# Attention masks as one-pass operands, and the gate as second factor of the normalising instruction

## The reference, cut to what matters

```python
# forgetting attention of the first layer, 128-wide heads
s = jnp.where(pos_k[None, :] <= pos_q[:, None], s, -jnp.inf)
p = jax.nn.softmax(s, axis=-1)
# selected attention: the 256 best keys of an index score
score = jnp.where(k_pos[None, None, :] <= q_pos[None, :, None], score, NEG_INF)
_, idx = lax.top_k(score, n_top)
# stick breaking: keys strictly before the query
mask = k_pos[None, :] < q_pos[:, None]
```

## Time and profile before

| | |
|---|---|
| median of 3 runs | 3654.83 us |
| the runs | 3655.05, 3650.49, 3654.83 us |
| the profiled execution | 3650.83 us |
| its span | 3649.1 us |
| PE, DVE, ACT, POOL busy | 3427.9, 1545.9, 1270.9, 321.0 us |
| mean granted clock of PE | 0.959 |

### The profile page before, as it was taken

One profiled execution on the slowest core, in us unless ns is written; L12 is line 12 of the kernel. 1 busy time (PEld: TensorE's weight loads), 2 busy tenths in 40 slices (PEclk: granted clock), 3 DMA queues, 4 the chain that ended last, 5 costly groups with the idle time before them and its releaser, 6 DMA issues. The chain is left out here.

```text
span 3649.1 us, 38273 instructions
## 1 busy us (share of the span) xinstructions
PE 3427.9 (94%) x15248; PEld 2718.3 (74%) x15248; DVE 1545.9 (42%) x2503; ACT 1270.9 (35%) x2183; POOL 321.0 (9%) x156
## 2 busy tenths in 40 slices
PE   7988889999999999999898999999999989889998
PEld 6755668877888888876675788878887757668886
DVE  4142431125333333444685533343334548663334
ACT  2324542233232322232455422232223235543222
POOL 0311214430000000023000000000000410000000
PEclk9998979999999999999899999999999979989999
DMA  3210213322333333331000233323333210023332
GB/s 130 81 42 23 70 35 104 98 87 87 98 98 93 100 97 98 97 103 58 30 1 24 86 95 97 98 82 98 98 96 103 87 35 1 1 70 98 97 95 75
DMA packets 76785, 279.60 MB, mean 77 GB/s; under 512 B 8768, under 2 KB 9024, under 8 KB 76352
## 3 DMA queue, kind: packets, MB, share of 16 engines
q1 hardware_dynamic: 76608, 277.16, 24.9%
HBM read 275.03 MB, written 2.10 MB: 76 GB/s over the span
## 5 line engine op out<-in xcount | busy, mean ns | idle before, releaser
L502 ACT ACTIVATE w_hi<-raw_slabs 128x1024 fp32r<-128x1024 f32 x496 | 524.4, 1058 | 1290.4 <-PE ps L542 1178.9
L517 DVE TENSOR_TENSOR w_lo<-raw_slabs,w_hi 128x1024 fp32r<-128x1024 f32 x376 | 459.9, 1223 | 750.1 <-ACT w_hi L502 750.0
L542 PE MATMUL ps<-in_hi,w_hi 128*128 128x512 f32 x1904 | 747.0, 392 | 9.6 <-DVE in_lo L819 9.6
L542 PE MATMUL ps<-in_hi,w_lo 128*128 128x512 f32 x1904 | 744.6, 391 | 0.0
L542 PE MATMUL ps<-in_lo,w_hi 128*128 128x512 f32 x1904 | 744.6, 391 | 0.0
L542 PE MATMUL ps<-parts,w_hi 128*128 128x512 f32 x2304 | 712.6, 391 | 7.7 <-PEq L378 7.7
L517 POOL TENSOR_TENSOR w_lo<-raw_slabs,w_hi 128x1024 fp32r<-128x1024 f32 x120 | 302.7, 2524 | 2569.5 <-ACT w_hi L502 2569.5
L542 PEld LDWEIGHTS ps<-parts,w_hi 128*128 128x128 f32 x2304 | 433.4, 188 | 99.4 <-issue 10.0
L542 PE MATMUL ps<-parts,w_lo 128*128 128x512 f32 x1152 | 449.3, 390 | 0.0
L542 PEld LDWEIGHTS ps<-in_hi,w_hi 128*128 128x128 f32 x1904 | 358.8, 188 | 91.0 <-DVE in_lo L819 9.2
L542 PEld LDWEIGHTS ps<-in_hi,w_lo 128*128 128x128 f32 x1904 | 359.3, 189 | 75.1
(11 more groups left out here) (259 smaller groups left out, 3569.6 us busy)
## 6 DMA issues: line engine op xcount, KB each, us to landing
raw_slabs<-weights SPq DMA_DIRECT2D x508, 512.0 KB, 3.5
big<-rope SPq DMA_DIRECT2D x2, 2304.0 KB, 9.2
x_resid<-xT SPq DMA_DIRECT2D x8, 256.0 KB, 4.5
outT<-x_resid SPq DMA_DIRECT2D x8, 256.0 KB, 2.0
const_cols<-consts SPq DMA_DIRECT2D x1, 836.0 KB, 9.3
scratch<-brow SPq DMA_DIRECT2D x1, 768.0 KB, 10.0
vector_cols<-vec SPq DMA_DIRECT2D x2, 45.5 KB, 9.8
vector_cols<-vec SPq DMA_DIRECT2D x1, 69.0 KB, 3.5
```

Source lines behind the costliest of these rows:

```text
L502: self.nc.scalar.activation(self.w_hi[:, m % SPLIT, :], self.raw[:, n % RAW, :], ACT.Copy)\
L517: (self.nc.gpsimd if i is None else self.nc.vector).tensor_tensor(self.w_lo[:, m % SPLIT, :], self.raw[:, n % RAW, :], self.w_hi[:, m % SP ...
L542: mm = k.nc.tensor.matmul(out, lhsT, rhs, start=(c == 0 and m == 0), stop=(last and m == 2))
```

## The change

A new SBUF tensor `masks` of four 128x128 float32r matrices holds the unit matrix and the causal, strict and compressed masks. DVE fills it once by four copies, at the start of the second phase with products (`lay_masks`). The mask matmul in `score` takes the unit matrix and the masks from it; L2231 writes the selection rows as float32r through `k.parts`, to the same place as before. The unit matrix in float32 stays for turns and for the other matmuls that use it. The gate product L1707 and its wait are gone; the normalisation of a gated unit has two factors, the reciprocal and the gate, both a column read from memory.

```diff
--- before.py
+++ after.py
@@ -223,6 +223,7 @@
                ("goes_on", T)):
     CONST.add(_n, _w)
 
+MASKS = ("ident", "causal", "strict", "cmp_neg")
 NORM_CONST = CONST.at["one"][0] + 1
 
 ROPE = Columns()
@@ -351,6 +352,7 @@
         self.w_lo = place("w_lo", [P, SPLIT, SLAB * P], F32R)
         sb = lambda name, shape: ctx.enter_context(nc.sbuf_tensor(name, shape, F32))
         self.const = sb("const_cols", [P, CONST.n])
+        self.masks = ctx.enter_context(nc.sbuf_tensor("masks", [P, 4 * P], F32R))
         self.vec = sb("vector_cols", [P, NVEC])
         self.stat = sb("stats", [P, 2, 64])
         self.ps = ctx.enter_context(nc.psum_tensor("ps", [P, 8, T], F32))
@@ -417,6 +419,18 @@
     def c(self, name, rows=P):
         at, n = CONST.at[name]
         return self.const[0:rows, at:at + n]
+
+    def mask(self, name):
+
+        at = P * MASKS.index(name)
+        return self.masks[:, at:at + P]
+
+    def lay_masks(self, dve):
+
+        for n, name in enumerate(MASKS):
+            at, w = CONST.at[name]
+            self.nc.vector.tensor_copy(self.mask(name), self.const[:, at + w - P:at + w])\
+                .then_inc(self.flag("masks_laid"), 1)
 
     def rope(self, name):
 
@@ -1606,7 +1620,7 @@
     for j, (lhsT, rhs) in enumerate(u.scores):
         nc.tensor.matmul(k.ps[:, bank, 0:w], lhsT, rhs, start=(j == 0), stop=False)
     n = u.mask.shape[1]
-    return nc.tensor.matmul(k.ps[:, bank, w - n:w], k.c("ident"), u.mask, start=False, stop=True)
+    return nc.tensor.matmul(k.ps[:, bank, w - n:w], k.mask("ident"), u.mask, start=False, stop=True)
 
 
 def turn(k, u, p, bank):
@@ -1662,14 +1676,13 @@
 
 
     nc = k.nc
-    scored, row_max, bias_scaled, expd, row_inv, row_gate, probs_ready, turned, laid, unit_done, stored = [
-        k.flag(n) for n in ("scored", "row_max", "bias_scaled", "probs_expd", "row_inv", "row_gate", "probs_ready",
+    scored, row_max, bias_scaled, expd, row_inv, probs_ready, turned, laid, unit_done, stored = [
+        k.flag(n) for n in ("scored", "row_max", "bias_scaled", "probs_expd", "row_inv", "probs_ready",
                               "turned", "laid", "unit_done", "stored")]
     n = len(units)
     ring, lag = 6, 3
     probs = lambda i: k.scr[:, i % ring, :]
     col = lambda kind, i: k.stat[:, kind, i:i + 1]
-    gates = [sum(1 for u in units[:i + 1] if u.gate is not None) for i in range(n)]
     scaled = [sum(1 for u in units[:i + 1] if u.scale != 1.0) for i in range(n)]
     groups = sum(1 for u in units if u.last)
     assert n <= 56
@@ -1704,9 +1717,9 @@
                     nc.vector.reciprocal(inv, inv).then_inc(row_inv, 1)
                     dve.wait_ge(row_inv, k.at(row_inv, i))
                     if u.gate is not None:
-                        nc.vector.tensor_tensor(inv, inv, u.gate, ALU.mult).then_inc(row_gate, 1)
-                        dve.wait_ge(row_gate, k.at(row_gate, gates[i - 1]))
-                    nc.vector.tensor_scalar(p, p, inv, None, ALU.mult).then_inc(probs_ready, 1)
+                        nc.vector.tensor_scalar(p, p, inv, u.gate, ALU.mult, ALU.mult).then_inc(probs_ready, 1)
+                    else:
+                        nc.vector.tensor_scalar(p, p, inv, None, ALU.mult).then_inc(probs_ready, 1)
 
         @block.scalar
         def _(act):
@@ -1722,7 +1735,7 @@
                     nc.scalar.activation(probs(i)[:, 0:u.width], k.ps[:, i % 3, 0:u.width], ACT.Exp, bias=col(0, i),
                                          scale=u.scale, accum_out=col(1, i)).then_inc(expd, 1)
                 lay_and_store(k, act, i - lag, n, units, turned, laid, unit_done, stored)
-    k.passed(scored=n, row_max=n, bias_scaled=scaled[-1], probs_expd=n, row_inv=n, row_gate=gates[-1], probs_ready=n,
+    k.passed(scored=n, row_max=n, bias_scaled=scaled[-1], probs_expd=n, row_inv=n, probs_ready=n,
              turned=n, laid=n, unit_done=n, stored=groups, top8=len(steps), top8_taken=len(steps),
              select_made=rows_done(steps))
 
@@ -2228,7 +2241,8 @@
         nc.vector.match_replace(s, best, s, TAKEN).then_inc(taken, 1)
         if t % TOP_STEPS == TOP_STEPS - 1:
             dve.wait_ge(taken, k.at(taken, t - first + 1))
-            nc.vector.tensor_scalar(s, s, TAKEN / 2, NEG, ALU.is_ge, ALU.mult).then_inc(k.flag("select_made"), 1)
+            nc.vector.tensor_scalar(k.parts[:, 32 + qb, 0:P * (qb + 1)], s, TAKEN / 2, NEG, ALU.is_ge, ALU.mult)\
+                .then_inc(k.flag("select_made"), 1)
 
 
 def share(steps, i, n):
@@ -2351,8 +2365,14 @@
     for j in range(4):
         jobs.append(F("mo", j, big[:, 36 + j, :], func=ACT.Sigmoid))
     gates = MlstmGates(k, small, i_row, f_fx, k.flag("taken"))
-    gemm_phase(k, jobs, scalar={2: gates.scalar}, vector=gates.vector)
+
+    def masks_and_gates(dve):
+        k.lay_masks(dve)
+        gates.vector(dve)
+
+    gemm_phase(k, jobs, scalar={2: gates.scalar}, vector=masks_and_gates)
     gates.passed()
+    k.passed(masks_laid=len(MASKS))
     mlstm_phase(k, tile(28), tile(32), value(0), lambda h: y(0, h))
     norm = RmsNorm(k, [[(y(0, h), y(0, h), k.v("ml_g", h), big[:, 36 + h, :])] for h in range(4)], "rms_eps", P,
                    bank=4)
@@ -2363,7 +2383,7 @@
 
 
     less_f = lambda h, n: [(k.c("negroot", 4)[:, h:h + 1].broadcast_to([4, P]), f_fx[0:4, 0:n])]
-    attention_phase(k, softmax_units(tile(28), tile(32), value(4), P, lambda qb: k.c("causal")[:, T - P:T],
+    attention_phase(k, softmax_units(tile(28), tile(32), value(4), P, lambda qb: k.mask("causal"),
                                      lambda h: y(1, h), P ** -0.5, extra=less_f))
     padded = big[:, 28:33, :].rearrange("p a b -> p (a b)")[:, 0:4 * (T + 3)].rearrange("p (j t) -> p j t", j=4)
     xc = lambda j: scr[:, j, :]
@@ -2457,7 +2477,7 @@
     select = lambda qb: tile(32 + qb)
     index_phase(k, lambda j: tile(11 + j), tile(13), lambda qb, h: v_tok(qb)[:, IW0 + h:IW0 + h + 1], select,
                 compress, both((dk,)))
-    causal = lambda qb: k.c("causal")[:, T - P:T]
+    causal = lambda qb: k.mask("causal")
     ys = lambda n: (lambda h: k.act[:, 2 * n + h // 2, :])
     two_heads = lambda base: (lambda h: tile(base + h // 2))
     one_half = lambda pair: (lambda h: tile(pair[h % 2]))
@@ -2474,9 +2494,8 @@
             more = dict(group=QB * h + qb, rows=(lo, lo + 64), out=ys(1)(h)[lo:lo + 64, P * qb:P * qb + P])
             gate = lambda b: gates[:, qb, 4 * b + h:4 * b + h + 1]
             qs = two_heads(14)(h)[:, P * qb:P * qb + P]
-            hidden = CONST.at["cmp_neg"][0] + wide * qb
             units.append(Unit([(qs, kc[h % 2])], wide, [vc], first=True, last=False, gate=gate(0),
-                              mask=k.const[:, hidden:hidden + wide], **more))
+                              mask=k.mask("cmp_neg")[:, wide * qb:wide * (qb + 1)], **more))
 
 
             for b, (kt, col) in enumerate(((ks, VS0), (kw, VW0))):
@@ -2485,11 +2504,11 @@
     attention_phase(k, units, select, range(*TOP_CUTS))
     units = softmax_units(two_heads(21), lambda h: tile(sk[h // 2][h % 2]),
                           lambda kb, h: v_tok(kb)[:, VB0 + P * (h // 2):VB0 + P * (h // 2) + P], 64,
-                          lambda qb: k.c("strict"), ys(3))
+                          lambda qb: k.mask("strict"), ys(3))
 
     stick_phase(k, units, select, range(TOP_CUTS[1], TOP_STEPS * (QB - 1)))
     units = softmax_units(two_heads(18), one_half(dk), shared(VD0), 64,
-                          lambda qb: causal(0) if qb == 0 else select(qb)[:, 0:P * (qb + 1)], ys(2))
+                          lambda qb: causal(0) if qb == 0 else k.parts[:, 32 + qb, 0:P * (qb + 1)], ys(2))
     attention_phase(k, units)
     norm = RmsNorm(k, [[(k.act[:, 2 * g + j, :], k.act[:, 2 * g + j, :], k.v("group_g", 2 * g + j), None)
                         for j in range(2)] for g in range(4)], "rms_eps", 256, parts=[x(c) for c in range(KD)])
```

## The result

The changed kernel took 3624.89 us (median of 4 runs, 3621.10 to 3626.25), the kernel before 3652.66 (4 runs, 3649.66 to 3655.05): a ratio of 0.9923, with a 95% interval from 0.9906 to 0.9940. The forecast was 3627.0. The profiled execution took 3623.74 us, with a span of 3621.9 and a granted clock of 0.957.

What follows compares the result with a forecast made beforehand. PE was taken to bound the first and selected attention, DVE the gated stage. Savings 2.4 + 0.6 + 11.0 + 11.6 = 25.6 us took 3650.83 to 3625.2; half the timed runs' 4.0 offset gave 3627, range 3614 to 3640.

Steps and rivals of the forecast that it cites:

- Selected attention, 5.8 each: Selected attention, twice: PE freed of 6.2 of 28 us by one-pass masks, taken as 5.8 us per layer.
- Gated stage, 5.5 each: Gated stage, twice: DVE is the bound and falls by 6.2 us, PE by 5.3; taken as 5.5 per layer.
- A narrow mask, 0.11 saved: Narrow masks on PE: two load-and-matmul pairs, 0.22 us, become one, 0.11 us.
- Second factor, +0.06: Gated normalisation on DVE: a second factor read from memory costs 0.06 us, 547 ns at 512 columns.
- MLA, 0.3 each: Attention with the first 14 top-k steps, twice: 1.8 us freed on PE, mostly hidden by DVE; 0.3 each.
- Stick-breaking, 0: Stick-breaking stage, twice: 1.8 us of PE freed behind a DVE kept busy by top-k; gain 0.
- First attention, 2.4: First attention, once: PE-bound, 16 one-pass masks, six at half clock and ten at full, save 2.4 us.
- Copies and selection rows, 0: Four added DVE copies hidden behind a wait for ACT, selection rows by the same six instructions: cost 0.
- Rival 1: A narrow one-pass matmul is no quicker, so only the 24 wide selection masks gain on PE: 3634 us; chance 0.20.
- Rival 4: The gated normalisation's second factor costs its upper bound: 2.6 us less saved per layer, 3632 us; chance 0.05.
- Rival 3: PE drops to its lower clock in the gated stage: 40 us lost per stage, 3667 us for one; chance 0.03.
- Rival 2: First attention's low-clock stretch ends at once, 3616 us, or lasts to the stage's end, 3653; chance 0.10 both ways.

Runs made afterwards that it cites:

- the gate alone: Kernel before with the gate as second factor of the normalisation, masks still plain float32; 3646.55 us, ratio 0.9982.
- one factor less: Changed kernel with the gate's factor left out of the normalisation, so its output differs; 3623.15 us (one run).
- the masks alone: Changed kernel with the separate gate product put back, all masks one-pass; 3637.59 us, ratio 0.9958.

## Why the prediction was right

**Step by step.** The forecast of 25.6 us for the profiled execution stands against 27.1, and the median against the median gives 27.8. That the whole came so near is luck in part: the first attention missed by 5.0 us, and MLA, stick-breaking and all else, for which the sum had 0.6, came to 7.4. Two readings were wrong without bearing on the sum: the attention stages together last 438 us and not some 390, and of DVE's 45.5 us in the stick-breaking stage 20.6 are top-k steps, which is not most of it.

- *Selected attention, 5.8 each:* 5.7 measured. It is PE's stage, and PE was relieved of what the sum says (0.63 us on a 512-wide mask: 1.72 - 1.09, each with its score). Right.
- *Gated stage, 5.5 each:* 5.5 measured. Right in size, but the step "so DVE bounds the gated stage and PE stands a fifth below it" failed. The gate alone brings 2.8 and not 5.5, and one factor less brings 1.4 of 2.9. PE's count of 60 of 72 us was an average over the stage, and the pieces of six units show what it hid: four of the seven follow DVE and three PE. The waits already had both signs, 2.5 us of DVE for PE and 5.7 of PE for DVE; I took the shorter for negligible. That the size was right is luck in part: the change happens to ease both engines, PE by 32 x 0.16 + 16 x 0.11 = 6.9 us per layer, DVE by the forecast's 6.2. By the same step the gate alone was expected to bring 5.4.
- *A narrow mask, 0.11 saved:* mis-sized for 128 columns, where 0.16 is saved in the tight places; right for 32. In the total it hardly matters: in the gated stage the masks alone bring 1.6 of the 6.9 us that PE is relieved of.
- *Second factor, +0.06:* 546 ns against 547 forecast. Right.
- *MLA, 0.3 each:* 0.5 and 0.9. Small either way.
- *Stick-breaking, 0:* shorter by 1.1 and 1.3, but with the same masks it lasted 52.9 to 55.5 us in the runs above, so this isn't shown to be the masks'. DVE's busy time there is 45.45 before and after. The length goes with the clock for the most part: over all ten kernels, the three of these stages with a clock column of 1.00 lasted 52.9 to 53.2 us, the seven with 0.88 55.1 to 55.5 (those between, 52.9 to 55.6), and the first one went from 0.94 to 1.00 with the change. All else moved by 3.6 us, though only the four copies were added there: the long stretch between the first attention and the MLA stage alone lasted 1423.9 us before and 1419.9 to 1422.8 in the other kernels.
- *First attention, 2.4:* 2.6 longer instead. Below.
- *Copies and selection rows, 0:* nothing in the rows speaks against it (the first attention starts at 303.8 us before and after); they weren't tried alone.

**The rivals.** Rival 1 (a narrow one-pass matmul is no quicker) falls: 0.92 us against 1.08. Rival 4 (the second factor at its upper bound) falls by the 546 ns. Rival 3 (low clock in the gated stage) did not happen in the changed kernel, whose clock was 1.00 there. It did happen with the masks alone, where PE had the same work and DVE more: 2.5 us in one layer, 0.7 in the other. So its mechanism is real, but its price here was far below the 40 us of a whole stage.

Rival 2 (the clock in the first attention moves) did happen, a part of the way to its second end: some 31 us at the low level against 21, and the stage 5 us above the forecast, the very mark set for this rival. Whether the one-pass masks lengthen that stretch isn't settled. The stage lasted 50.8, 52.5 and 57.3 us in three kernels with plain masks, and 53.4 in three with one-pass masks; the spread of the former holds the latter. What is shown is the part of the four-row product in the low clock: by the clock columns it was low for 20 to 34 us in the six kernels with that product, and for 3 to 7 in the four without it. What sets the length among the six stays open.

## What to carry to other kernels

Cut a stage into pieces of a few units before calling one engine its bound: two engines that are late by turns look like one bound with a spare fifth, and then each half of a change alone brings less than its part of the whole. The price of a one-pass matmul behind a multi-pass one is read from one score's start to the next other product, not from the mask's own record. And where PE is busy throughout at half its clock, look at the products' rows: padding them with zeros took 18.5 us off a 53.4 us stage here, some third of that by the products' own pace, though only 13.0 arrived in the total.

## What the runs showed of the hardware that was not expected

- PE was busy for 4.00 of 4.00 us, stretch after stretch, and its granted clock stayed at the lower of its two levels (1.2 of 2.4 GHz) for some 31 us, while the stage had products of 4 rows; it then rose with the same products still running. With the same products at 128 rows, zeros in 124, it rose after some 3 us (53.4 us became 34.9). The Trainium skill (TensorE: Matmul & The Clock Gate, section What's actually happening) says that the default state is throttled and that activity releases it; here full busy time in the records did not for those 31 us.
- At the full clock, a product of 4 rows between products of 128 cost 0.39 us more than the same product padded to 128 rows, at every width from 128 to 512 columns (512: 2.17 against 1.78 us with its score and mask).
- In the kernel with the masks alone the clock fell to the lower level within the gated stage, around stretches with PE busy 2.80 and 3.08 of 4.00 us; it stayed at 1.00 in the changed kernel at 2.84 of 4.00 once (1870 to 1874), and at the start of the same gated stage at 2.68 and 2.84 (1808 to 1816).
- A 128-wide one-pass matmul costs 0.06 us behind a multi-pass product, with its weight load hidden, though its record shows 0.31 to 0.62.
